# Seven-product feed-forward rounds: weight sums made in DRAM by adding transfers, and wider VectorE instructions

## What is computed

```
def swiglu(h, w1, w3, w2):
    return (jax.nn.silu(h @ w1) * (h @ w3)) @ w2

def _half_ffn(h, g, m, k, w1, w3, w2):
    y = swiglu(_modulate(h, g, m, k), w1, w3, w2)
    return h + (0.5 * m[:, :, 3 * k + 2] * y).astype(h.dtype)
```

## Time and profile before

| | us |
|---|---|
| median of three runs | 2976.67 |
| profiled execution, its own time | 2973.72 |
| its span | 2971.9 |
| PE busy | 2735.2 |
| VectorE (DVE) busy | 2147.9 |
| ScalarE (ACT) busy | 1170.8 |
| GpSimd (POOL) busy | 370.5 |

### The profile page before, as it was taken

The page is one execution under the profiler, slowest core; times in us unless marked ns, Lnnn a source line. Parts: engine busy times, 40 slices in busy tenths (PEclk is TensorE's granted clock), DMA queues, the critical chain, the costliest instruction groups (busy, mean ns, idle before and its releaser), DMA issues.

```text
span 2971.9 us, 38986 instructions
## 1 busy us (share of the span) xinstructions
PE 2735.2 (92%) x15048; PEld 2503.1 (84%) x15048; DVE 2147.9 (72%) x3319; ACT 1170.8 (39%) x1921; POOL 370.5 (12%) x252
## 2 busy tenths in 40 slices
PE   5989888899998999989898998888989989899999
PEld 5988888899986899888898998888989876688887
DVE  6987888884558687888878878787788757653333
ACT  3233232345547643332323433223234866542222
POOL 2010010120002520110101201001012420100000
PEclk8999999999999999999999999999999999999999
DMA  7223334222130033233242232332322110133333
GB/s 279 93 85 97 120 92 133 74 68 64 50 70 2 1 114 107 86 91 117 93 132 73 66 104 86 102 114 88 108 74 90 57 50 22 43 91 93 97 101 101
DMA packets 76118, 262.18 MB, mean 88 GB/s; under 512 B 8352, under 2 KB 9504, under 8 KB 75040
## 3 DMA queue, kind: packets, MB, share of 16 engines
q1 hardware_dynamic: 58080, 192.59, 21.2%
q10 hardware_dynamic: 17856, 67.12, 7.3%
HBM read 257.58 MB, written 2.10 MB: 87 GB/s over the span
## 4 chain that ended last, share of the span: by engine, by line
PE 53%; DVE 29%; issue 9%; DMA 5%; ACT 2%; POOL 0%; ACTq 0%; DVEq 0%; SPq 0%; POOLq 0%
PE banks L610 10%; PE banks L612 9%; PE banks L614 9%; PE banks L617 5%; PE banks L621 5%; PE banks L619 5%; DMA raw<-in_w 5%; DVE banks L1931 4%; DVE wl L2007 4%; DVE ssum L2000 4%; DVE tmp L2061 2%; DVE hl L2012 1%; DVE wl L1926 1%; DVE tmp L2204 1%; PE banks L1141 1%
## 5 line engine op out<-in xcount | busy, mean ns | idle before, releaser
L1270 ACT ACTIVATE wh<-raw 128x1024 fp32r<-128x1024 f32 (+3 forms) x230 | 219.9, 957 | 766.0 <-PE banks L614 447.2
L1926 DVE TENSOR_TENSOR wl<-raw,wh 128x1024 fp32r<-128x1024 f32 (+3 forms) x248 | 273.6, 1103 | 202.7 <-ACT wh L1270 167.4
L698 PE MATMUL banks<-xh,wh 128*128 128x384 f32 x864 | 303.3, 351 | 116.1 <-DVE wl L2007 115.8
L1931 DVE SCALAR_TENSOR_TENSOR banks<-mraw,scb 128x1024 f32<-128x1024 f32 x240 | 305.1, 1271 | 6.2 <-DMA mraw<-in_wmn 1.0
L610 PE MATMUL banks<-hh,wh 128*128 128x384 f32 x1056 | 273.0, 339 | 24.3 <-DVE wl L1926 24.1
L699 PE MATMUL banks<-xl,wh 128*128 128x384 f32 x864 | 293.4, 340 | 0.0
L700 PE MATMUL banks<-xh,wl 128*128 128x384 f32 x864 | 293.3, 340 | 0.0
L698 PEld LDWEIGHTS banks<-xh,wh 128*128 128x128 f32 x864 | 165.1, 191 | 146.1 <-DVE wl L2007 146.1
L612 PE MATMUL banks<-hl,wh 128*128 128x384 f32 x1056 | 271.6, 338 | 0.0
L614 PE MATMUL banks<-hh,wl 128*128 128x384 f32 x1056 | 271.4, 338 | 0.0
L610 PE MATMUL banks<-xh,wh 128*128 128x384 f32 x880 | 230.8, 343 | 21.5 <-DVE xl L2196 12.1
(11 more groups left out here) (419 smaller groups left out, 6074.6 us busy)
## 6 DMA issues: line engine op xcount, KB each, us to landing
raw<-in_w SPq DMA_DIRECT2D x184, 512.0 KB, 3.6
mraw<-in_wmn ACTq DMA_DIRECT2D x120, 512.0 KB, 3.6
raw<-in_w SPq DMA_DIRECT2D x72, 384.0 KB, 3.1
raw<-in_abin SPq DMA_DIRECT2D x24, 512.0 KB, 3.6
raw<-in_cdin SPq DMA_DIRECT2D x20, 512.0 KB, 3.6
raw<-in_w SPq DMA_DIRECT2D x16, 448.0 KB, 3.3
raw<-in_w SPq DMA_DIRECT2D x24, 256.0 KB, 2.6
mini<-in_wmn SPq DMA_DIRECT2D x9, 512.0 KB, 14.8
```

The lines of the kernel that those rows point to most:

```text
L698: pe.matmul(thirds(bank), W, rh(k), start=(k == 0), stop=False)
L1270: act.activation(wh[slot][:, 0:nk * P], raw[slot][:, 0:nk * P], ACT.Copy).then_inc(hi_done, 1)
L1926: dve.tensor_tensor(wl[slot][:, 0:nk * P], raw[slot][:, 0:nk * P], wh[slot][:, 0:nk * P].bitcast(F32), ALU.subtract).then_inc(lo_done, 1)
L1931: return dve.scalar_tensor_tensor(B67[:], tile, 1.0, scv[:, s, :], ALU.mult, ALU.mult, accum_out=out)
```

## The change

1. The four weight sums of all six chunks of a round are made in DRAM, in a new internal tensor `sums`, by eleven transfers that GpSimd issues (`weight_sums`): three plain copies and eight that add to their target, in four steps, each step behind the landing of the one before. The w3 blocks enter with the other sign (S1 as it was, then A11 + A21, A11 + S1, and A12 with all of these), and a factor of -1 in the hidden product makes it good. GpSimd issues the transfers of the first four rounds behind the squares of the first norm, those of the next four behind the squares of the third norm, and the last round's behind those of the fourth. `seven_pool` is gone.
2. SyncE loads a chunk's blocks in four transfers: A11 (256 KB, its own buffer a11), two sums into raw[0] and two into raw[1] (512 KB each), A12 with A22 (512 KB, its own buffer a2). Before the first sums of a round it waits for that round's sums, on the same queue as all other weight loads.
3. VectorE no longer adds weights. Its splits of S3 and S4 are one instruction of 1024 columns; the two subtractions of P5, the hidden product and the hidden low half take both halves of the tokens at once; the gate's other half is added by VectorE from PSUM, in place of ScalarE's copy and GpSimd's addition. The order of splits is S34, A22, S1, A11, A12, S2. The pair of dots of a chunk is parted in two places, and the dots of the last down tile move into the first chunk of the next round.
4. A12 has its split halves in wh[0] and wl[0], A11 in buffers of its own, and in the last chunk of a round A12 takes A11's. The load of a round's first w2 tile waits for S2's low half (before: A12's), the second for S34's.

The core of the diff (without the removed lines, up to the last part):

```diff
+        a11 = at("a11", [P, 512], w)
+        a2 = at("a2", [P, 2, 512], w + 512)
+        wah = at("wah", [P, 512], w + 3 * 512, F32R); w += 4 * 512
...
+        u23 = at("u23", [P, 2, T // 2], TB + 2 * T)
+        ghf = at("ghf", [P, 2, 2, T // 2], TB)
+        gs, hs = ghf[:, 0], ghf[:, 1]
...
+        W_SRC = {"A11": a11[:], "S1": raw[0][:, 0:512], "S2": raw[0][:, 512:D], "S34": raw[1][:], "A12": a2[:, 0], "A22": a2[:, 1]}
+        W_HI = {"A11": wah[:], "S1": wh[0][:, 0:512], "S2": wh[0][:, 512:D], "S34": wh[1][:], "A22": weh[:],
+                "A12": wh[0][:, 512:D], "last A12": wah[:]}
+        W_LO = {"A11": wal[:], "S1": wl[0][:, 0:512], "S2": wl[0][:, 512:D], "S34": wl[1][:], "A22": wel[:],
+                "A12": wl[0][:, 512:D], "last A12": wal[:]}
...
+            def load_a11(f, g, i):
+                s, row = seven_pair(f, g, i), 2 * (f * FC + first_chunk(f, g) + i)
+                if s:
+                    sp.wait_ge(w_lo, w_count(s - 1, "A11"))
+                sp.dma_start(a11[:], dr["w13"][row, :, 0:512]).then_inc(a11_landed, 16)
+
+            def load_a2(f, g, i):
+                s, row = seven_pair(f, g, i), 2 * (f * FC + first_chunk(f, g) + i)
+                if s:
+                    sp.wait_ge(w_lo, w_count(s - 1, "A12"))
+                sp.dma_start(a2[:], dr["w13"][row:row + 2, :, 512:D].rearrange("q p c -> p q c")).then_inc(a2_landed, 16)
+
+            def load_sums(f, g, i, q):
+                t, s = up_tile(f, g) + 2 * i, seven_pair(f, g, i)
+                if i:
+                    sp.wait_ge(w_lo, w_count(s - 1, ("S2", "S34")[q]))
+                else:
+                    sp.wait_ge(lo_done, PLAIN[t - 2 + q] + 1)
+                    if q == 0:
+                        sp.wait_ge(sum_landed, sums_landed(f, g))
+                src = dr["sums"][SEVEN_ROUNDS.index((f, g))][:, i, 2 * q:2 * q + 2, :]
+                sp.dma_start(raw[q][:].rearrange("p (b c) -> p b c", b=2), src).then_inc(raw_landed[q], 16)
...
+                        if seven(f, g):
+                            if i:
+                                load_a11(f, g, i)
+                            load_sums(f, g, i, 0)
+                            load_sums(f, g, i, 1)
+                            if i:
+                                load_a2(f, g, i)
...
                 pe.wait_ge(w_lo, w_count(s, "A11"))
                 pe.wait_ge(psum_free[1], t // 2 - 1)
+                product(P1_BANK[i % 2], W_HI["A11"], W_LO["A11"], *tokens(0, 0)).then_inc(p_done, 1)
+                pe.wait_ge(w_lo, w_count(s, "S1"))
                 pe.wait_ge(psum_free[0], t // 2)
                 if i == 0:
                     pe.wait_ge(t_ready, 5 * (f + 1))
+                product(P5_BANK, W_HI["S1"], W_LO["S1"], *tokens(0, 1)).then_inc(p_done, 1)
                 pe.wait_ge(w_lo, w_count(s, "S2"))
+                product(P6_BANK, W_HI["S2"], W_LO["S2"], *sums(0)).then_inc(p_done, 1)
                 if s:
                     pe.wait_ge(comb_set, comb_count(s - 1, "C21"))
+                pe.wait_ge(w_lo, w_count(s, "S34"))
+                product(P7_BANK, W_HI["S34"][:, 0:512], W_LO["S34"][:, 0:512], *sums(1)).then_inc(p_done, 1)
                 pe.wait_ge(psum_free[1], t // 2)
+                product(P3_BANK, W_HI["S34"][:, 512:D], W_LO["S34"][:, 512:D], *tokens(4, 1)).then_inc(p_done, 1)
                 pe.wait_ge(w_lo, w_count(s, "A12"))
                 pe.wait_ge(half_set, 3 * s + 1)
+                product(P1_BANK[i % 2], W_HI[p2], W_LO[p2], *tokens(4, 0)).then_inc(mm_done, 1)
+                pe.wait_ge(w_lo, w_count(s, "A22"))
+                pe.wait_ge(comb_set, comb_count(s, "U3"))
+                product(P7_BANK, W_HI["A22"], W_LO["A22"], *sums(2)).then_inc(mm_done, 1)
...
+                if name == "A12":
+                    act.wait_ge(p_done, 5 * s + (1 if last else 3))
+                elif name in ("A22", "S34"):
                     act.wait_ge(mm_done, t)
                 elif i == 0:
+                    act.wait_ge(mm_done, t - KC if name == "A11" else t - 1)
                 elif name == "S2":
                     act.wait_ge(mm_done, t - 1)
                 else:
+                    act.wait_ge(p_done, 5 * (s - 1) + {"A11": 1, "S1": 2}[name])
...
+                dve.tensor_tensor(hs[:, 0], u23[:, 1], P7_BANK, ALU.subtract).then_inc(comb_set, 1)
                 dve.wait_ge(comb_set, comb_count(s, "C21"))
                 dve.wait_ge(half_set, 3 * s + 3)
+                dve.scalar_tensor_tensor(hs, gs, -1.0, hs, ALU.mult, ALU.mult).then_inc(comb_set, 1)
+
+            def hidden_lo(f, g, i):
+                s = seven_pair(f, g, i)
+                dve.wait_ge(hf_hi, s + 1)
+                dve.tensor_tensor(halves(hl[:, i, :]), halves_of(hs), halves(hh[:, i, :].bitcast(F32)), ALU.subtract
+                                  ).then_inc(h_ready, 1)
...
             def seven_act(f, g, i):
                 n = GROUPS[f][g]
                 t, s = up_tile(f, g) + 2 * i, seven_pair(f, g, i)
                 last = i == n - 1
+                weight_hi(f, g, i, "S34")
                 weight_hi(f, g, i, "A22")
                 if i:
+                    hidden_hi(f, g, i - 1)
                 act.wait_ge(p_done, 5 * s + 1)
+                act.wait_ge(psum_free[1], t // 2)
                 act.activation(p1[:], P1_BANK[i % 2], ACT.Copy).then_inc(half_set, 1)
                 if not last:
                     weight_hi(f, g, i + 1, "S1")
+                    weight_hi(f, g, i + 1, "A11")
+                if i == 0:
+                    next_mods(f, ("down", g - 1, KC - 1))
+                weight_hi(f, g, i, "A12")
                 if last:
                     act.wait_ge(raw_landed[0], 16 * (t // 2 + 1) + 16)
+                    act.wait_ge(p_done, 5 * s + 3)
                     act.activation(wh[0][:, 0:n * P], raw[0][:, 0:n * P], ACT.Copy).then_inc(hi_done, 1)
+                act.wait_ge(comb_set, comb_count(s, "C12"))
+                act.activation(gs[:, 1], gs[:, 1], ACT.Silu).then_inc(half_set, 1)
                 if last:
                     act.wait_ge(raw_landed[1], 16 * (t // 2 + 1) + 16)
+                    act.wait_ge(p_done, 5 * s + 5)
                     act.activation(wh[1][:, 0:n * P], raw[1][:, 0:n * P], ACT.Copy).then_inc(hi_done, 1)
+                else:
+                    weight_hi(f, g, i + 1, "S2")
+                act.wait_ge(psum_free[1], t // 2 + 1)
+                act.activation(gs[:, 0], gs[:, 0], ACT.Silu).then_inc(half_set, 1)
+                next_mods(f, ("up", first_chunk(f, g) + i))
+                if last:
+                    hidden_hi(f, g, i)
...
             def seven_dve(f, g, i):
                 n = GROUPS[f][g]
+                t, s, ch = up_tile(f, g) + 2 * i, seven_pair(f, g, i), first_chunk(f, g) + i
                 last = i == n - 1
                 if i:
                     last_quarter(f, g, i - 1)
+                weight_lo(f, g, i, "S34")
                 weight_lo(f, g, i, "A22")
                 if i:
+                    hidden_lo(f, g, i - 1)
+                else:
+                    dot_mods(f, ("down", g - 1, KC - 1))
+                dot_half(f, ("up", ch), 0)
                 dve.wait_ge(half_set, 3 * s + 1)
                 dve.wait_ge(p_done, 5 * s + 3)
+                dve.tensor_tensor(u23[:, 0], p1[:], P6_BANK, ALU.subtract).then_inc(comb_set, 1)
                 if not last:
                     weight_lo(f, g, i + 1, "S1")
+                    weight_lo(f, g, i + 1, "A11")
+                weight_lo(f, g, i, "A12")
                 dve.wait_ge(p_done, 5 * s + 4)
+                dve.wait_ge(comb_set, comb_count(s, "U2"))
+                dve.tensor_tensor(u23[:, 1], u23[:, 0], P7_BANK, ALU.add).then_inc(comb_set, 1)
+                dve.wait_ge(comb_set, comb_count(s, "U3"))
+                dve.wait_ge(h_ready, f * FC + ch)
+                dve.tensor_tensor(ghf[:, :, 1], u23[:], P5_BANK.unsqueeze(1).to_broadcast([P, 2, T // 2]), ALU.subtract
+                                  ).then_inc(psum_free[0], 1)
                 if last:
                     split_lo(t + 2, 0, n)
+                dve.wait_ge(p_done, 5 * s + 5)
+                dve.wait_ge(psum_free[0], t // 2 + 1)
+                dve.tensor_tensor(gs[:, 1], gs[:, 1], P3_BANK, ALU.add).then_inc(comb_set, 1)
+                dot_half(f, ("up", ch), 1)
+                dve.wait_ge(mm_done, t + 1)
+                dve.tensor_tensor(gs[:, 0], p1[:], P1_BANK[i % 2], ALU.add).then_inc(psum_free[1], 1)
+                if last:
+                    split_lo(t + 3, 1, n)
+                    last_quarter(f, g, i)
+                    hidden_lo(f, g, i)
                 else:
                     weight_lo(f, g, i + 1, "S2")
...
+            def weight_sums(f, g):
+
+                r, n = SEVEN_ROUNDS.index((f, g)), GROUPS[f][g]
+                row = 2 * (f * FC + first_chunk(f, g))
+                tile = dr["w13"][row:row + 2 * n].rearrange("(i q) p c -> q p i c", q=2)
```

(22 more changed lines are left out.)

206 lines of the change are left out of this document (67 added, 139 removed).

## The result

The changed kernel takes 2804.27 us, the median of four runs (2799.36 to 2808.61), against 2975.28 (2971.89 to 2978.64) for the kernel before, timed beside it. The ratio is 0.9425, with a 95% interval of 0.9405 to 0.9445. Its profiled execution took 2802.96 us, with a span of 2801.2.

A forecast was written before the change was run, and what follows sets the result against it. PE was taken to wait for VectorE's work and the raw[0] loop. Nine rounds at 91.1 us (820 for 976) save 156, less 5 at the start: 2976.7 - 151 = 2826 us, range 2793 to 2960.

The forecast's parts named there:

- the loop through raw[0]: Old chunk: A12 in raw[0] split last, raw[0] reloaded only then, next chunk's S2, A11, S4 wait; VectorE idle 1.78 us.
- The bound: Nine seven-product rounds: 976 us now, 793 us if PE never stalls, so at most 183 us to gain.
- The pitch of a chunk: PE's 84 matmuls in a chunk without stalls: 14.69 us, against 16.79 us in a usual chunk.
- Entry and exit: Allowance at each of nine rounds' ends: 1.5 us at entry and 0.5 us at exit.
- my walk: VectorE's new order through a chunk, timed from its start T: S34 split by T+2.9, S2 by T+14.1.
- The collision: Old chunk: VectorE's S4 and a 384-wide product slowed beside GpSimd's two additions, about 1.9 us a chunk.
- Landings: Allowance in the rounds for loads landing slower beside the sums' transfers: 1 us per round.
- my list: Signs to look for: among them raw[0] landing under 6 us; loads landing beyond 8 us would prove it wrong.
- transfers share the engines: Rival, chance 0.17: in the rounds raw[0] lands in 8 us or more, PE waits 1.5 us a chunk, 2907 us.
- The start: Sums' transfers slow the start-up loads before the first round: 5 us, bounds 0 and 15.
- The sums' own time: GpSimd's eleven transfers for a round's sums: 90 us, free up to about 122 us a round.
- 131 us for 90: First round's sums: from GpSimd's first squares ending at 30 us until wanted at about 161 us, for 90 us of transfers.

The follow-up runs named there:

- b_one: Kernel before, with GpSimd's additions cut to 8 columns (layer one), VectorE's sums likewise (layer two), A12 in its own buffer (layer three): 2898.23 us.
- a_back1: a_nosums with extra additions per chunk: GpSimd's in layer one, GpSimd's and VectorE's in layer two, VectorE's in layer three: 2788.96 us.
- a_nosums: Changed kernel without the transfers that make the sums; as many bytes loaded from the weights themselves: 2780.23 us, ratio 0.9350.
- a_copy: Changed kernel with its eight adding transfers a round as plain copies of the same blocks: 2801.38 us in one run.
- a_late: Changed kernel with two more plain 1536 KB copies a round, which the adding transfers wait for: 2846.14 us, ratio 0.9588.

## Why the prediction was right, and where it was off

It gave 2826 us, and 2822.7 for the profiled execution; that took 2803.0. The mechanism was the one named: PE waited for VectorE, by its work and by the loop through raw[0] together, and with both relieved PE is the bound. The sizes were off as follows, and the nearness of the total owes something to luck, since the errors run both ways.

1. *The bound.* "183 us is all that any edit of them can return": 168 of them came. PE's waits inside the products were 146.1 us in 94 times before, and 16.6 us in 13 times are left.
2. *The pitch of a chunk.* 14.69 us from the first chunk of a round; it is 14.58, 6 us over 54 chunks.
3. *Entry and exit.* I put 1.5 + 0.5 us a round, 18 us in all. In the rounds of layer three they are nil: 87.48 us hold six chunks and nothing else. This is the largest error. No row of the prediction shows the 1.5, and its own walk through a round's first chunk had a loss of only 0 to 1 us.
4. *VectorE.* 11.7 to 12.3 us a chunk were worked out, 12.16 measured. The order of my walk (S34 at T+2.9, U2 at T+6.5) is that of the timeline above.
5. *The collision.* 1.9 us a chunk; the edit of b_one gave 1.70. In the changed kernel about half of it, put back in a_back1, cost nothing.
6. *Landings.* I put 1 us a round, 9 us in all. It is 20.9, all in the six rounds beside the sums: there the loads of raw land in 7.2 to 8.3 us in the median, over the 6 that my list asked for and about the 8 that it called wrong, and ScalarE's waits for them reach 7.2. The rival "transfers share the engines" is thus real, and its condition (8 us) was nearly met, at a quarter of its 81 us: 0.6 us a chunk over 36 chunks and not 1.5 over 54. Its second way, that GpSimd's issuing slows VectorE as its additions did, is not seen. VectorE's splits of 1024 columns in the first layer's rounds, beside the sums, and in the third's, without them:

```profile
L2062 DVE TENSOR_TENSOR wl<-raw,wh 128x1024 fp32r<-128x1024 f32 x18 | 21.9, 1218 | 2.3 <-ACT wh L1404 2.3
```

```profile
L2062 DVE TENSOR_TENSOR wl<-raw,wh 128x1024 fp32r<-128x1024 f32 x18 | 21.9, 1218 | 0.2 <-ACT wh L1404 0.2
```

7. *The start.* 5 us; the first round starts 0.1 us later than before (166.59 against 166.50) and 0.9 later than in a_nosums, too little to tell from none (a_copy, with shorter transfers, started it at 170.17 in its one execution).
8. *The sums' own time.* 90 us a round, and 117 to 127 measured. Ninety was chosen between bounds of 45 and 130 by the nearest rows; the upper one, the rate of a lone load, was the better guide. The steps of plain copies in a_copy take 39.9 us (145.23 to 185.08) behind 35.8 us of larger copies; with twice the price for the steps this is 115.6, near what was measured. The rule that the prediction cites (the Trainium skill, Collectives: The Full Stack, The bandwidth ceiling), that a reduction moves half of what a copy moves, agrees with the 2.06; the page has it for collectives. The error cost little, since the sums count only from about 122 us a round, and some 9 us of room were left before the first round (its sums had landed by 149.22 and were loaded at 157.94); a_late shows what some 15 us more a round do. That was partly luck: the margin was far thinner than 131 us for 90.

Items 2 and 3 (24 us), 7 (5) and 2.7 us by which the rest of the kernel became shorter make 31.5 us faster than forecast, item 6 makes 11.9 slower: 19.6 of the 19.7 us between forecast and profile.

## What to carry to other kernels

When one engine is the bound and several edits each relieve it, their gains do not add: here 31, 15 and 28 us a layer alone came to 52 to 58 together, and two of the three gave 42 to 53. Nor are they the same in the new kernel as in the old: there each cost of VectorE alone was hidden, and the late buffer cost 72.6 us. Before a block of work is moved to transfers, put every allowance of the old stretch (its entry, its exit, its waits) through the new order instead of carrying it over, and give an adding transfer twice a copy's time. Where such transfers have a deadline, try them in the stretches in which the loads are few: in single profiled executions that took 8.7 us off the rounds, and making the transfers a third shorter took off 4.0.
